# A hybrid decoder step with routed experts on one core: tokens dealt to tiles of 128, 128 and 32 rows instead of three of 96, and a different routing chain and tail

## What is computed

```python
def layer(x, pos0, conv_buf, pool_buf, ...):
    h = rmsnorm(x, g_mix)
    p = h @ w_in                                   # 2048 -> 3072
    v, gate, u = p[..., :D_CONV], p[..., D_CONV:2 * D_CONV], p[..., 2 * D_CONV:]
    yc, new_conv = conv_mixer(v, gate, conv_buf, w_dw, b_dw, ln_g, ln_b)
    yp, new_pool = pool_mixer(u, pool_buf, pos0, w_pool, pool_scale)
    x = x + jnp.concatenate([yc, yp], axis=-1) @ w_out
    x = x + hier_moe(rmsnorm(x, g_ffn), w_rg, b_rg, w_re, b_re, w_gate, w_up, w_down)
    return x, new_conv, new_pool

def hier_moe(h, ...):                              # 4 groups x 8 experts, D_EXPERT = 512
    glog = hf @ w_rg + b_rg;  g_sel = argmax(glog);  p_g = softmax(glog)[g_sel]
    elog = hf @ w_re + b_re                        # only the 8 of the chosen group count
    top_v, top_i = lax.top_k(elog_sel, 2);  w_top = softmax(top_v) * p_g
    for e in range(32):
        a = silu(hf @ w_gate[e]) * (hf @ w_up[e])
        y = y + gates[:, e:e + 1] * (a @ w_down[e])
```

## Time and profile before

| | us |
|---|---|
| median of 3 runs | 1377.18 (1371.01 to 1377.28) |
| the profiled execution | 1375.67 |
| its span | 1373.8 |
| TensorE busy in the span | 1269.0 |
| VectorE busy | 348.6 |
| ScalarE busy | 109.0 |
| GpSimd busy | 108.2 |

### The profile page before, as it was taken

One profiled execution on the slowest core, in us unless ns is written; L12 is line 12 of the kernel. 1 busy time (PEld: TensorE's weight loads), 2 busy tenths in 40 slices (PEclk: granted clock), 3 DMA queues, 4 the chain that ended last, 5 costly groups with the idle time before them and its releaser, 6 DMA issues.

```text
span 1373.8 us, 16203 instructions
## 1 busy us (share of the span) xinstructions
PE 1269.0 (92%) x6492; PEld 711.5 (52%) x6492; DVE 348.6 (25%) x695; ACT 109.0 (8%) x251; POOL 108.2 (8%) x164
## 2 busy tenths in 40 slices
PE   8999998999999988888998998999898899889886
PEld 7777776777864444443443444444344444434421
DVE  4499963111241010110101011110101101010217
ACT  2100014000200000000000000000000000000012
POOL 2211164000000100000000000000000000000000
PEclk9999999999999999999999999999999999999997
DMA  9444425565549999999999999999999999999895
GB/s 240 167 133 159 136 92 174 207 245 183 214 168 392 425 427 428 426 429 426 428 427 427 429 425 428 426 426 412 427 418 427 428 425 421 423 424 408 354 324 149
DMA packets 82485, 464.59 MB, mean 338 GB/s; under 512 B 8079, under 2 KB 50191, under 8 KB 56195
## 3 DMA queue, kind: packets, MB, share of 16 engines
q1 hardware_dynamic: 76784, 455.89, 82.3%
q0 software_dynamic: 5392, 7.86, 1.8%
q10 hardware_dynamic: 283, 0.48, 0.1%
HBM read 456.67 MB, written 20.80 MB: 348 GB/s over the span
## 4 chain that ended last, share of the span: by engine, by line
DMA 42%; PE 40%; issue 7%; DVE 5%; POOL 3%; SPq 1%; ACT 1%; DVEq 0%; POOLq 0%
DMA arena<-in_w_up_dram 40%; PE bank L729 20%; PE bank L568 11%; DVE arena L1003 3%; PE bank L707 3%; PE bank L750 3%; DMA stage<-in_w_down_dram 2%; POOL arena L1378 1%; SPq L400 1%; DMA arena<-expert_rows 1%; PE bank L517 1%; PE bank L653 0%; POOL arena L1387 0%; DVE arena L1229 0%; PE bank L801 0%
## 5 line engine op out<-in xcount | busy, mean ns | idle before, releaser
L729 PE MATMUL bank<-arena,stage 128*64 128x512 f32 x1920 | 442.1, 615 | 59.1 <-DMA arena<-in_w_up_dram 59.1
L729 PEld LDWEIGHTS bank<-arena,stage 128*64 128x64 f32 x1920 | 146.8, 142 | 347.6 <-issue 311.6
L568 PE MATMUL bank<-arena,stage 128*128 128x288 f32 x1280 | 315.2, 407 | 2.9 <-ACT arena L880 1.5
L568 PEld LDWEIGHTS bank<-arena,stage 128*128 128x128 f32 x1280 | 241.8, 190 | 69.1 <-ACT arena L880 2.0
L707 PEld LDWEIGHTS bank<-x1w,x1r 96*128 96x128 f32 x1536 | 173.9, 192 | 26.1 <-issue 26.1
L707 PE MATMUL bank<-x1w,x1r 96*128 96x128 f32 x1536 | 180.0, 277 | 0.8 <-DVE x1w L1118 0.8
L1257 DVE TENSOR_TENSOR a_sb<-sl_sb,bank 128x256 f32<-128x256 f32 x32 | 19.3, 604 | 498.3 <-ACT sl_sb L919 498.3
L750 PE MATMUL bank<-arena,aT 128*64 128x512 f32 x512 | 113.4, 595 | 8.5 <-ACT aT L921 8.5
L1003 DVE SCALAR_TENSOR_TENSOR arena<-arena,wdw 128x256 f32<-128x256 f32 x240 | 103.0, 504 | 0.0
L1395 POOL DMA_INDIRECT expert_rows<-ysb,cur_d x31 | 30.3, 978 | 856.1 <-DVE ysb L1271 827.9
L1271 DVE TENSOR_SCALAR ysb<-bank,wslot 128x512 f32<-128x512 f32 x31 | 23.3, 751 | 255.6 <-PE bank L750 255.6
(11 more groups left out here) (239 smaller groups left out, 493.2 us busy)
## 6 DMA issues: line engine op xcount, KB each, us to landing
arena<-in_w_gate_dram SPq DMA_DIRECT2D x48, 2048.0 KB, 14.3
arena<-in_w_up_dram SPq DMA_DIRECT2D x48, 2048.0 KB, 21.3
arena<-in_w_down_dram SPq DMA_DIRECT2D x30, 2048.0 KB, 17.5
xT<-in_w_down_dram SPq DMA_DIRECT2D x15, 2048.0 KB, 20.5
stage<-in_w_down_dram SPq DMA_DIRECT2D x15, 2048.0 KB, 21.9
arena<-in_w_gate_dram SPq DMA_DIRECT2D x16, 1536.0 KB, 14.4
arena<-in_w_up_dram SPq DMA_DIRECT2D x16, 1536.0 KB, 21.8
stage<-in_w_in_dram SPq DMA_DIRECT2D x11, 2048.0 KB, 8.0
```

The lines of the kernel that those rows point to most:

```text
L568: last = pe.matmul(ps[bank][:, 0:NTOK], wsl[a][:, k, cc * P:(cc + 1) * P], rhs[:, k, :], start=(n == 0), stop=(n == KT - 1))
L729: mm = pe.matmul(ps[4 + s][BLK * h:BLK * (h + 1), :], xgT[:, k, BLK * s:BLK * (s + 1)], w[:, :, 256 * h:256 * (h + 1)], start=(k == 0), st ...
```

## The change

Five things.

1. **Tiles.** Tokens are dealt to tiles of TS = (128, 128, 32) rows with starts T0 = (0, 128, 256): two tiles of prompt tokens and one of the sample tokens. x is loaded in three DMAs, two of 128 rows and one of 32. All routing tensors get 128 partitions. The matmuls over tiles keep their number.
2. **Fillers.** `stay_awake` is called with 7, 3, 3 and 8 in the start instead of 12, 7, 6 and 10, and with 18, 4 and 2 in the routing instead of 30 and 12.
3. **Routing.** In the last round of the projection `rows_and_router(3, 2)` stands between the eighth and ninth matmul of the last dense block. The group mask is made in one instruction less. The rank matmuls run on `oh1` and on `oh2` separately, the first beside VectorE's work on `oh2`. The first pair's `hot` is built straight from the rank within experts 0 and 1, 64 columns each, times the sum of the one-hots and the row's factor; the slot numbers come later, for the next pair.
4. **First pair.** Of the four quarters of select for the next pair, one stands behind expert 0 and three behind expert 1, instead of two and two. VectorE takes the second quarter of inputs of pair 0 one step earlier.
5. **Tail.** The prompt tiles have 128 rows; VectorE adds both copies itself, and TensorE only places the last expert. The sample tokens are handled as quarters: token t's columns 512q to 512q + 511 stand on partition 32q + t (`yq`, `x1q`, `gfq`), so that one instruction of 512 columns does the 32 rows. The sum of squares over the four partitions of a token is a matmul with `same_token`. The DMAs of the quarters are written with q outermost, 4 x 32 x 512.

```diff
-TR = 96
-TT = NTOK // TR
-LASTP = SEQ - 2 * TR
+TS = (128, 128, 32)
+T0 = (0, 128, 256)
+TT = len(TS)
+QC = D // 4
-AWAKE_START = (12, 7, 6)
-AWAKE_SCALE = 10
+AWAKE_START = (7, 3, 3)
+AWAKE_SCALE = 8
-AWAKE_ROUTE = (30, 12)
+AWAKE_ROUTE = (18, 4, 2)
...
+            for t in range(2):
+                sp.dma_start(x1r[:, t, :], x_prompt[0, T0[t]:T0[t] + P, :]).then_inc(x_in[t], 16)
+            sp.dma_start(x1r[0:NS, 2, :], xs_rows).then_inc(x_in[2], 16)
...
+                    if between and n == KT // 2:
+                        between()
...
+                    elif last and q == 3:
+                        dense(q % 2, a, q % 2, mixT, between=lambda: rows_and_router(3, 2)).then_inc(o_mm, 1)
+                        break
...
+            for n, oh in enumerate((oh1, oh2)):
+                pe.wait_ge(pick_ready, n + 1)
+                pe.matmul(ps[6][:, 0:TT * NE], earlier[:, :], oh[:, :, :].rearrange("p t e -> p (t e)"), start=(n == 0), stop=False)
...
+                if n == 0:
+                    stay_awake(AWAKE_ROUTE[1])
...
-                        for b in (2 * s, 2 * s + 1):
+                        for b in ((0,), (1, 2, 3))[s] if first else (2 * s, 2 * s + 1):
                             select(i + 1, b)
...
+            picked, rank2 = r4d[:, :, 0:2], r4c[:, :, 0:2]
+            link(dve.tensor_tensor(picked, oh1[:, :, 0:2], oh2[:, :, 0:2], ALU.add))
+            link(dve.tensor_tensor(picked, picked, rs[:, :, None].to_broadcast([P, TT, 2]), ALU.mult))
...
-            take(ra[:, :, :])
-            one_hot(0)
+            link(dve.tensor_copy(rank2, picked_rank[:, :, 0:2]))
+            for e in range(2):
+                for t in range(TT):
+                    ins = dve.tensor_scalar(hot[:, t, BLK * e:BLK * (e + 1)], iof[:, 0:BLK], rank2[:, t, e:e + 1], picked[:, t, e:e + 1],
+                                            ALU.is_equal, ALU.mult)
+            ins.then_inc(hot_ready, 1)
...
+            sp.wait_ge(gu_used, 4 * (NE - 1) + 2)
+            for t in range(2):
                 for c in range(2):
+                    sp.dma_start(yg[:, t, c, :], by_token[T0[t]:T0[t] + P, c * D:(c + 1) * D]).then_inc(yg_in[t][c], 16)
+            sp.wait_ge(gu_used, 4 * NE)
             for c in range(2):
+                sp.dma_start(yq[:, c, :], by_token[SEQ:NTOK, c * D:(c + 1) * D].rearrange("t (q d) -> q t d", q=4)).then_inc(yq_in[c], 16)
...
+            pe.wait_ge(act_over, 1)
+            pe.wait_ge(first_sum, 1)
...
+            pe.wait_ge(yq_in[1], 16)
+            pe.wait_ge(part_added, 1)
+            pe.matmul(ps[0][:, :], ident[:, :], yq[:, 1, :], start=True, stop=False)
...
             def add_residual(t):
...
+                link(dve.tensor_tensor(a3, a3, x1p[:, t, :, :], ALU.add))
+                dve.wait_ge(yg_in[t][1], 16)
+                dve.tensor_tensor(yg[:, t, 0, :], yg[:, t, 0, :], yg[:, t, 1, :], ALU.add).then_inc(first_sum, 1)
```

More of the change, by code:

```diff
@@ L17 @@
 NTOK = SEQ + NS
-TR = 96
-TT = NTOK // TR
-LASTP = SEQ - 2 * TR
+TS = (128, 128, 32)
+T0 = (0, 128, 256)
+TT = len(TS)
+assert sum(TS) == NTOK and T0[2] == SEQ and TS[2] == NS
+QC = D // 4
 CT = 8
@@ new lines, in hybrid_decoder_step @@
+        den = sb("den", [P, TT, 1])
+        wt = sb("wt", [P, 2, TT])
+        sel = sb("sel", [P, TT, NE])
+        ra = sb("ra", [P, TT, NE])
+        rc = sb("rc", [P, TT, NE])
+        oh1 = sb("oh1", [P, TT, NE])
+        oh2 = sb("oh2", [P, TT, NE])
+        rank = sb("rank", [P, TT, NE])
+        cnt = sb("cnt", [P, NE])
+        rk_i = sb("rk_i", [P, (TT + 1) * NE], I32)
+        rq = sb("rq", [P, TT + 1, NE])
+        rc2 = sb("rc2", [P, TT, NE])
+        cs = sb("cs", [P, 2, NE])
+        slot = sb("slot", [P, 2, TT])
@@ L283, in hybrid_decoder_step @@
         zero_out = sem("zero_out")
-        yg_in = [[sem(f"yg_in{t}{c}") for c in range(2)] for t in range(TT)]
+        yg_in = [[sem(f"yg_in{t}{c}") for c in range(2)] for t in range(2)]
+        yq_in = [sem(f"yq_in{c}") for c in range(2)]
+        act_over = sem("act_over")
+        x1q_ready = sem("x1q_ready")
+        squared2 = sem("squared2")
+        total_mm = sem("total_mm")
+        token_ready = sem("token_ready")
         pvT_mm = sem("pvT_mm")
@@ L559, in taps_and_states, with dense @@
                     last.then_inc(hist_mm, 1)
-            def dense(bank, a, cc, rhs, order=range(KT), late=None, each=None):
+            def dense(bank, a, cc, rhs, order=range(KT), late=None, each=None, between=None):
                 for n, k in enumerate(order):
@@ L676, in _ @@
             projection(0, first=True)
-            with pe.Fori(1, 4) as o:
+            with pe.Fori(1, 3) as o:
                 projection(o)
+            projection(3, last=True)
             pe.wait_ge(act_chain, 4 * TT)
@@ L910, in _ @@
             act.activation(ex[:, :, :], dl[:, :, :], ACT.Exp).then_inc(exp_done, 1)
+            act.wait_ge(row_evac, 4 * TT + 1)
+            for q in range(4):
+                act.copy(x1q[NS * q:NS * (q + 1), :].rearrange("r (p k) -> r p k", k=KT), x1p[0:NS, 2, 32 * q:32 * (q + 1), :]).then_inc(x1q_ready, 1)
             def pair(i, first=False, last=False):
@@ L1177, in _ @@
             ch.step(dve.tensor_copy(slot_i[:, :], slot[:, :, :].rearrange("p c t -> p (c t)")))
-            for b in range(1, 4):
+            for b in range(2, 4):
                 inputs(0, b)
```

378 lines of the change are left out of this document (190 added, 188 removed).

## The result

The changed kernel takes **1394.49 us** (median of four runs, 1388.65 to 1400.79), the kernel before 1377.18. The ratio is 1.0135, 95% interval 1.0116 to 1.0154. The forecast was 1359.3 us, faster than before. The profiled execution took 1398.07 us, its span 1396.0.

A forecast was written before the change was run, and what follows sets the result against it. The long middle was taken as bound by weight bytes over DMA rate. Gains of 2.8 + 4.3 + 2.8 + 8.0 = 17.9 us, taken from the median 1377.18, gave 1359.3 us, range 1352 to 1368.

The forecast's parts named there:

- The change moves none of those bytes: Long middle (expert loop): it costs its bytes over its rate, 425 GB/s over 854 us, which the change leaves alone.
- The condition I gave at the end: Sign of being wrong: x loads near 250 GB/s, up-weight waits lengthening or vanishing, or VectorE's contiguous add over 3 us.
- Start, 2.8: Loads of x on 128 partitions run at about 428 GB/s, so VectorE's third square starts at 10.5; gain 2.8 us.
- Rival A: Slow loads are not about 96 partitions: start -0.7 instead of +2.8, tail's VectorE 4.5 later; 1367.3 us, chance 0.11.
- Routing, 4.3: Moved rows, split rank matmuls and shorter one-hot steps bring select earlier; gain 4.3 us, bounds 3.3 to 4.8.
- Pair 0, 2.8: One select block fewer behind expert 0's gates, so expert 2's gate load issues earlier; gain 2.8 us, bounds 0 to 3.1.
- Tail, 8.0: Faster expert-row loads, VectorE's contiguous adds and sample quarters shorten the end of the kernel; gain 8.0 us.
- D: Tail's quarter transfers crawl on one or a few engines: 14 us worse, 1373.3, no change; chance 0.06.
- C: With fewer fillers the clock drop may meet select and gates: at most 1.8 us worse, 1361.1; chance 0.07.
- E: TensorE stays at 1.2 GHz from the routing through pair 0: slower than before, up to 1409 us; chance 0.03.
- The chance of slower, 0.03: Whole kernel: the probability given to a measured time slower than before, 0.03, against 0.89 for faster.

The follow-up runs named there:

- e11: The changed kernel run again without an edit; 1397.27 us, ratio 1.0156.
- e9: The kernel of e12 with pair 0's select blocks back in their old order, two behind expert 0's gates and two behind expert 1's; 1365.49 us.
- e12: The kernel of e8 run a second time, in more rounds; 1363.73 us.
- e1: The changed kernel with select reading the third tile on all 128 partitions, rows 32 to 127 being zeros; 1369.55 us.
- e2: The changed kernel with each bank's four 32-row select matmuls first, then the eight of the tall tiles; 1372.01 us.
- e8: The kernel of e1 plus wider third-tile weights in the projection, fillers near 217 us with regrouped slot-table matmuls, and a reworked tail; 1362.34 us.
- e4: The kernel before with all three token tiles cut to 32 rows in select, leaving 192 tokens out; 1384.51 us in one run.
- e3: The kernel before with the third token tile cut from 96 to 32 rows in select, leaving 64 tokens out; 1468.06 us.

## Why the prediction was wrong, point by point

- **"The change moves none of those bytes", so the middle keeps its length.** This is the step that failed. It takes for granted that the weights stay the limit, and so puts what TensorE does in the loop at nothing. The select matmuls have their number, but I never priced them with the third tile at 32 rows. The condition I gave at the end came true word for word: the waits for up weights vanished, 59.1 us to 0.0. What the runs showed in its place: each of the 16 changes of height in a stretch costs 0.181 us, 2.89 us a stretch, and TensorE becomes the limit. Price: 14.5 us in the loop and, in pair 0, two and a half stretches (two of 48 records, one of 24) at 2.89, 7.2 us. The earlier trace rows held the warning: 71 us of idle over 28 experts, 2.5 us an expert, was all the cover TensorE had, and 0.5 of it (the wait for the transposed activation) was not to be had.
- **Start, 2.8.** The rate on 128 partitions was right in kind: 401 GB/s in 4 to 6 us (265 before), but 343 in 6 to 9; the first weight loads are issued from 2.19 us on, and that they are why is not shown. The third square began at 11.58 where 10.5 was forecast, the first scaling at 17.05 where 15.9 was: 1.7 us. The clock drop near 220 us took 1.6 of these in the profiled execution, so 0.1 came through; without the drop (e11) it was 1.6. Rival A is out.

```profile
9.24 2.29 DVE L1014 CUSTOM_DVE_ANT_0 arena<-x1r 128x2048 f32<-128x2048 f32 x1 [0.97 <-DMA x1r<-in_x_prompt_dram]
11.58 2.28 DVE L1014 CUSTOM_DVE_ANT_0 arena<-x1r 32x2048 f32<-32x2048 f32 x1
...
6.00:9.00 3.00, 3.00 (x17) 3.00 (x18) 2.27 (x2) 1.49 (x3) 0.00 (x0) 1.00 0.99 343
```

  These are rows of after that answer to the earlier trace rows: the second square waits 0.97 us for its tile.
- **Projection, not mentioned.** 15 blocks of 0.22 us, 3.3 us lost. The prediction priced the rows and router matmuls of the last block only.
- **Routing, 4.3.** From the last residual to the first select it is 12.15 us (16.37 before), but the moved rows put the last residual back by 1.0, not 0.6 (9.9 us behind the one before it, where the other blocks take 8.84). The gain is 3.2, just under the lower bound. The shortened steps came as forecast; 0.7 was lost to hops and the six one-hots (1.43 where 1.2 was forecast).
- **Pair 0, 2.8.** Right in size by e9 and e12 (2.7), and outweighed in the changed kernel: 7.2 of select, 7.6 of low clock and 0.8 in the slot tables, less 2.7, is 12.9 of the 13.0 in the table. What makes the clock fall in the first select is open: e1 and e2 tie it to the switching select, and no more.
- **Tail, 8.0.** 5.3 came. Up to the last add the forecast holds within 0.3 us (the partial sums begin 18.0 us after SyncE's load, forecast 17.9). Two terms were mis-sized. The final gains landed late, a wait that I had put at nothing, and the last store took 6.3 us to the end instead of 4.9. The rows of after for both (the wait stands in brackets; the span ends at 1396.0):

```profile
1380.04 0.16 DVE L1278 TENSOR_TENSOR va<-ss,ssp 128x1 f32<-128x1 f32 x1 [1.66 <-DMA arena<-in_g_final_dram]
...
1389.67 0.60 SPq L521 DMA_DIRECT2D out_dram<-arena  x1
```

  1.7 + 1.4 = 3.1 is a little more than the shortfall of 2.7; the chain between the two ran 0.4 faster than costed. VectorE's contiguous add took 2.29, as forecast (2.2). Of the rivals D was right in kind, a transfer on few engines, with 1.4 us instead of 14.
- **Rivals.** None named the mechanism that decided. C saw clock drops as at most 1.8 us; they cost 1.6 near 220 and 7.6 in pair 0. E named a low clock through pair 0 and gave it 3 in 100, since "TensorE is as busy as before". By the records it was, and the clock was low all the same. The chance of slower, 0.03, was far too small for a sum whose largest item, the middle, rested on one count of matmuls.

## What to carry to other kernels

Uneven tiles are not free on TensorE: a 32-row remainder between 128-row tiles costs two changes of height for each use, 0.36 us here, where zeros up to 128 rows cost nothing. If the short operand must stay, put its matmuls together. And where a loop is bound by loads, count the other engine's idle time for one turn first; an edit to each turn is covered only up to that, less the waits that are not for loads.

The combined kernel (changed tiles, padded select, wider third tile in the projection, fillers ahead of the last pools, tail in four transfers) is the fastest here, 0.9897 of before (0.9876 to 0.9918) in e8 and 0.9914 (0.9901 to 0.9928) in e12.

## What the runs showed of the hardware that I had not expected

- A change between 128- (or 96-) and 32-row operands costs TensorE 0.18 us at full clock in select (5.62 us a stretch with none, 8.51 with 16), and 0.10 in the slot tables' matmuls of 42 columns. For a change of weights' width between 128 and 32 columns the figures give 0.02 us net, 0.05 as an estimate.
- The granted clock can fall to half behind stretches with 32-row operands though TensorE's records leave no gap: 0.50 in 386 to 392 us of e4, and a mean of 0.90 in the loop windows of e3 and e4. It need not: the kernel after and e2 read 32-row operands all through that window at 0.99. e3 lost 92 us by reading fewer rows.
- A gap of 2.7 us near 217 us was followed by a low clock (0.52 in 220 to 222 us) in one execution of the changed kernel and not in another (1.00).
